# Gate and up weight chunks of a two-stage MoE layer: one 8 KB run per partition instead of four of 2 KB

## The reference, cut to what matters

```
h  = x + gmlp(rmsnorm(x) * norm_mix)
hn = rmsnorm(h) * norm_ffn
for each expert e:   y[e] = (silu(hn[rows_e] @ w_gate[e]) * (hn[rows_e] @ w_up[e])) @ w_down[e]
out = rmsnorm(h + sum_e weight_e * y[e]) * norm_final
```

## Time and profile before

| what | value |
|---|---|
| median of 3 executions | 1353.35 us (1352.79 to 1354.3) |
| span of the profiled execution | 1351.2 us |
| TensorE busy with matmuls | 937.8 us, 69% of the span |
| VectorE, ScalarE busy | 277.7 us and 293.4 us |
| bytes moved by DMA | 463.38 MB |
| mean rate over the span | 343 GB/s |

### The profile page before, as it was taken

The page is one execution under the profiler, slowest core; times in us unless marked ns, Lnnn a source line. Parts: engine busy times, 40 slices in busy tenths (PEclk is TensorE's granted clock), DMA queues, the critical chain, the costliest instruction groups (busy, mean ns, idle before and its releaser), DMA issues.

```text
span 1351.2 us, 18292 instructions
## 1 busy us (share of the span) xinstructions
PE 937.8 (69%) x7326; PEld 508.5 (38%) x7327; DVE 277.7 (21%) x471; ACT 293.4 (22%) x492; POOL 17.2 (1%) x53
## 2 busy tenths in 40 slices
PE   7999999995675766576666656656655656656664
PEld 6788788882232322132222223222222323223221
DVE  4454755442001000200020002000200110010003
ACT  5444555433111111111111110111111111111113
POOL 1100000002000000000000000000000000000000
PEclk9999999998777787777678788778988888688677
DMA  8776756765799999999999999999999999999993
GB/s 276 271 242 231 232 186 210 272 212 212 284 398 398 378 398 398 398 370 397 397 364 395 396 397 368 398 397 397 369 396 397 397 376 396 397 397 365 399 398 161
DMA packets 182361, 463.38 MB, mean 343 GB/s; under 512 B 7992, under 2 KB 8080, under 8 KB 165456
## 3 DMA queue, kind: packets, MB, share of 16 engines
q1 hardware_dynamic: 181520, 458.26, 90.7%
q0 software_dynamic: 624, 2.94, 0.6%
q10 hardware_dynamic: 80, 0.02, 0.0%
HBM read 459.09 MB, written 2.10 MB: 341 GB/s over the span
## 4 chain that ended last, share of the span: by engine, by line
PE 40%; SPq 22%; DMA 21%; issue 10%; DVE 3%; ACT 3%; DVEq 0%; ACTq 0%
SPq L234 22%; DMA late<-in_e_w_down 18%; PE bank L922 18%; PE bank L1062 8%; PE bank L1104 5%; PE bank L1046 5%; PE bank L1079 2%; DMA ring<-in_e_w_up 1%; DMA w_raw<-in_a_w_in 1%; PE bank L1051 1%; DVE xeT L847 1%; ACT w_router L578 1%; ACT y L590 1%; DVE w_lo L636 1%; PE bank L1010 1%
## 5 line engine op out<-in xcount | busy, mean ns | idle before, releaser
L1062 PE MATMUL bank<-ring,xeT 128*32 128x256 f32 x3584 | 237.6, 429 | 41.5 <-DVE xeT L847 31.3
L1046 PE MATMUL bank<-h,sel 128*32 128x512 f32 x512 | 115.6, 1053 | 180.4 <-issue 178.0
L1062 PEld LDWEIGHTS bank<-ring,xeT 128*32 128x32 f32 x3584 | 144.9, 123 | 127.9 <-issue 85.7
L922 PE MATMUL bank<-w_hi,xT_hi 128*128 128x512 f32 x384 | 155.3, 404 | 5.6 <-DVE w_lo L636 3.5
L922 PE MATMUL bank<-w_hi,xT_lo 128*128 128x512 f32 x384 | 151.5, 394 | 0.0
L922 PE MATMUL bank<-w_lo,xT_hi 128*128 128x512 f32 x384 | 151.1, 394 | 0.0
L636 DVE TENSOR_TENSOR w_lo<-w_raw,w_hi 128x1024 fp32r<-128x1024 f32 x96 | 119.2, 1242 | 132.5 <-ACT w_hi L431 132.3
L431 ACT CAST w_hi<-w_raw 128x1024 fp32r<-128x1024 f32 x96 | 100.9, 1051 | 140.9 <-PE bank L922 135.5
L590 ACT COPY y<-bank 32x512 f32<-32x512 f32 x128 | 73.8, 577 | 204.3 <-PE bank L1079 201.9
L1046 PEld LDWEIGHTS bank<-h,sel 128*32 128x32 f32 x512 | 19.5, 157 | 252.7 <-issue 250.2
L847 DVE TENSOR_TENSOR xeT<-bank,cols_T 128x512 f32<-128x512 f32 x32 | 22.1, 692 | 421.9 <-PE bank L1051 421.9
(11 more groups left out here) (148 smaller groups left out, 421.5 us busy)
## 6 DMA issues: line engine op xcount, KB each, us to landing
ring<-in_e_w_gate SPq DMA_DIRECT2D x112, 1024.0 KB, 14.4
ring<-in_e_w_up SPq DMA_DIRECT2D x112, 1024.0 KB, 14.9
ring<-in_e_w_down SPq DMA_DIRECT2D x64, 1024.0 KB, 14.8
late<-in_e_w_down SPq DMA_DIRECT2D x64, 1024.0 KB, 15.7
w_raw<-in_a_w_in SPq DMA_DIRECT2D x64, 512.0 KB, 3.7
w_raw<-in_a_w_out SPq DMA_DIRECT2D x32, 512.0 KB, 4.0
v<-in_e_w_gate SPq DMA_DIRECT2D x16, 1024.0 KB, 14.4
v<-in_e_w_up SPq DMA_DIRECT2D x16, 1024.0 KB, 14.7
```

Source lines behind the costliest of these rows:

```text
L922: ins = pe.matmul(Z[parity][t][:, :], a[:, k, toks], b[:, hc % 2, j, :], start=(k == 0 and part == 0), stop=(k == KD - 1 and part == 2))
L1046: ins = pe.matmul(XE[j * CAP:(j + 1) * CAP, :], sel[:, t, :], h[:, t, j * NBLK:(j + 1) * NBLK], start=(t == 0), stop=(t == NT - 1))
L1062: ins = pe.matmul(GU[c * CAP:(c + 1) * CAP, 0:256], xeT[:, kk, kc, :], slot_of(2 * kc + c // 2, q % 2)[:, half:half + 256], start=(kc == 0 ...
```

## The change

The source of a gate or up chunk is cut so that partition p receives the four adjacent rows 4p to 4p+3 of its 512 rows (8 KB in one run in memory), not rows p, 128+p, 256+p and 384+p (four runs of 2 KB). The destination is the same 8 KB per partition. So that features and weights meet, piece b of the transposed tokens must hold features 4p+b of each group of 512: the four transposes take every fourth column of xe, beginning at b, and norm_ffn is loaded a second time, as g_rows, in the matching order. The router keeps the old order.

```diff
+        g_rows = sb("g_rows", [P, NQ, KC])
...
+        g_rows_in = sem("g_rows_in")
...
                 w, k = (e_gate, e_up)[c % 2], c // 2
-                return w[0, e, k * KC * P:(k + 1) * KC * P, :].rearrange("(j p) n -> p j n", p=P)
+                return w[0, e, k * KC * P:(k + 1) * KC * P, :].rearrange("(p j) n -> p j n", j=KC)
...
             pool.dma_start(b_router[:, NGRP:NR], r_b_exp.partition_broadcast(P)).then_inc(router_in, 16)
+            pool.dma_start(g_rows[:, :, :], norm_ffn.rearrange("o (j p b) -> p (o j) b", j=NQ, b=KC)).then_inc(g_rows_in, 16)
             pool.wait_ge(lo_done, HC)
...
+                dve.wait_ge(g_rows_in, 16)
                 dve.wait_ge(s.xeT_ps, n + 1)
 
                 dve.tensor_tensor(xeT[:, :, :, :], TR[:, :].rearrange("p (b j c) -> p b j c", b=KC, j=NQ),
-                                  g_ffn.rearrange("p (j b) -> p b j", b=KC).unsqueeze(3).to_broadcast([P, KC, NQ, CAP]),
+                                  g_rows[:, :, :].rearrange("p j b -> p b j").unsqueeze(3).to_broadcast([P, KC, NQ, CAP]),
                                   ALU.mult).then_inc(s.xeT, 1)
...
                 for b in range(KC):
-                    ins = pe.transpose(TR[:, b * P:(b + 1) * P], xe[:, b * P:(b + 1) * P], ident[:, :])
+                    ins = pe.transpose(TR[:, b * P:(b + 1) * P], xe.rearrange("p (c b) -> p b c", b=KC)[:, b, :], ident[:, :])
                 ins.then_inc(s.xeT_ps, 1)
```

## The result

The changed kernel takes 1310.68 us (median of 4, 1307.6 to 1312.82), the kernel before 1353.07 us (4, 1350.22 to 1354.3). The ratio is 0.9686, interval 0.9666 to 0.9707: 3.1% faster, 42.4 us. Forecast were 1317.7 us and -35.6 us, range 1303 to 1330. The profiled execution took 1309.32 us for a span of 1307.4 us; the span of before was 1351.2 us, so the two traces differ by 43.8 us.

A forecast was written before the change was run, and what follows sets the result against it. The expert stage was taken to be bound by weight transfers, with DMA not the limit at group boundaries. Terms -49.5 + 11.6 + 2 + 0.3 = -35.6 us gave a span of 1315.6 and a time of 1317.7 us, range 1303 to 1330.

The forecast's parts named there:

- (1): Expert stage: gate and up chunks in 8 KB runs save 0.21 us each, -49.5 us; upper bound 0.23 us each.
- (2): Seven group boundaries: TensorE's path stays 29.6 us while the queue runs dry 1.65 us sooner; 11.6 us given back.
- (3): Four transposes per pass read xe with a step: 2 us at the boundaries; loads between 142 and 568 ns.
- that rival's 12 us: Strided transpose loads at the 7 boundaries cost their upper bound, 12 us instead of 2: 1328 us; chance 0.08.
- (4): New norm_ffn load on GpSimd's queue: issue hidden, its runs mix with the mixer's halves; +0.3 us, -0.5 to +0.9.
- (5): VectorE's new wait for g_rows: data there 300 us earlier, so nothing; the tail is unchanged too.
- (6): SP's queue: long issues become short, over 3 us vanish; issue to landing gets longer; worth nothing.
- The boundary doesn't bind: Group boundaries: loss comes from DMA engines' unequal ends, so 11.6 us aren't given back; about 1304 us; chance 0.10.
- Doesn't do what it says: Gate and up chunks still go out in 2 KB pieces, rate stays 387: 1353 us plus at most 2; chance 0.07.
- The slower rival: TensorE's start-up gaps grow behind larger descriptors; if both boundary gaps double, 75 us more, 1393 us; chance 0.05.

The follow-up runs named there:

- experiments 1 to 4: Changed kernel with 2 KB runs 1358.52 us, 4 KB 1323.51, 1 KB 1424.71; parts singly: source order 1311.15, all but it 1357.95, g_rows unused 1353.37.
- experiment 5: TensorE's scatter moved from before the next group's first gather to behind that pass's gate and up matmuls: kernel before 1344.36 us, kernel after 1293.89 us.
- experiment 4: Parts singly: changed source order alone 1311.15 us; all of the change but that order 1357.95; kernel before plus g_rows loaded, waited for, unused 1353.37.

## Why the prediction was right, point by point

*(1) 8 KB runs, -49.5 us.* Right in kind and place (experiments 1 to 4) and nearly in size. The rates are 387 and 420 as forecast; but from landing to landing, the median of a gate or up chunk in the trace went from 2.706 to 2.485 us, 0.221 us and not 0.206. Over 240 chunks that is 3.5 us more than the sum had. The prediction's own upper bound has a slip: 421 against 387 GB/s is 0.22 us per chunk and not 0.23, and its low end of 1303 us goes with 0.22.

*(2) The boundaries give back 11.6 us.* Right in mechanism, somewhat too large. In the stretch of 28 experts 224 chunks, each 0.221 us shorter, would have brought 49.5 us, and it became 39.9 us shorter: 9.6 us were given back, with the strided transposes in it. The windows say 10; experiment 5 returns 8.1 of it by the times (some 7 us uncertain) and 5.8 by the traces. Why it is less than the whole 1.65 us each time isn't shown. It isn't that TensorE's path became shorter (207.7 us in sum over the seven boundaries, 205.6 before), although TensorE's gaps, 31 ahead of the gathers and 7 ahead of the scatters, did shrink. They sum to 167.4 and 34.6 us after the change:

```profile
PE bank L1050 <- issue: 167.4, 31, 6.7
PE bank L1108 <- issue: 34.6, 7, 5.6
```

and to these before:

```profile
PE bank L1046 <- issue: 178.0, 31, 6.8
PE bank L1104 <- issue: 38.0, 7, 5.6
```

*(3) Strided transposes, 2 us.* The load takes 216 ns, between the ends of 142 and 568, so the Trainium skill's note (SBUF — State Buffer, Specifications) that each new 16-byte line costs agrees with the row; it costs half a load more, and the four elements' time of the upper bound isn't reached. The time of it is 1.6 to 7.0 us by experiment 4 with the old source order, so that rival's 12 us are shut out there; in the changed kernel the boundary paths are 2.0 us longer in sum than with the source order alone, one execution each. That is the forecast's 2 us, but not well settled, and 0.6 us of it at most is the loads' own time; the forecast had no term for the rest.

*(4), (5) The new load and the wait, 0.3 us and nothing.* Nothing speaks against them: g_rows alone is -0.1 us, between -3.7 and +2.8. The issue took GpSimd 0.75 us:

```profile
26.39 0.75 POOL L365 DMA_DIRECT2D g_rows<-in_norm_ffn  x1
```

*(6) SP.* Issues over 3 us became rare, 7 of the expert chunks' 384 where there were 59, but did not vanish as forecast: the one at 624.40 still took 6.08 us. The time from issue to landing became longer, as forecast.

In the span, the sum's 35.6 us came out as 43.8, 8.2 more. Term (1) has 3.5 us of that. The 240 chunks come to 53.0 us, so 9.2 us were lost again in all, where terms (2), (3) and (4) together had 13.9: the other 4.7 us. How these divide among the three isn't shown beyond what stands above. The forecast of the time was 7 us too high, inside its range, because the two errors went the same way.

*The rivals.* "The boundary doesn't bind" fell by the 9.6 us given back and by experiment 5: the boundary does bind. "Doesn't do what it says" fell by the packets. The slower rival fell in its sign: with all descriptors at 8 KB, the waits ahead of L1050 are 5.40 us in the mean where they were 5.74, and those ahead of the scatters 4.94 where they were 5.43. The rule that 512 B are enough for line rate (the Trainium skill, DMA: Bandwidth & Descriptors, Specifications) doesn't hold for this stream: 1 KB runs reach 350 GB/s, 83% of what 8 KB runs do.

## What to carry to other kernels

Where weights stream at the DMA engines' limit, give each partition one long run by dealing adjacent rows to it, and permute the other operand to match; four strided transposes a pass cost little against it, at most 7 us of 42 here. Price it from two windows of the trace that move runs of different length, not from the share of busy time, which was at or over 1 in both. Then look for the stretches where something else sets the pace: there a faster stream only empties the buffers sooner, and moving work off that path was worth more after the change (16.8 us) than before it (9.1).

## What the runs showed that I had not expected

- The cost of a run is linear from 1 to 8 KB: about 9 ns and 37.8 ns per KB on each DMA engine (46.7, 84.9, 160.8, 312 ns).
- One boundary of the kernel after moved only 272 GB/s in its window. TensorE's granted clock there was 0.68, against 0.82 to 0.93 in the windows of the others, and the path from last landing to next issue took 31.6 us instead of 28.6 to 30.0. A boundary on TensorE's path pays for the clock; a DMA-bound stretch doesn't, as the two windows at 420 GB/s with a granted clock of 0.51 and 0.89 show.
- With the scatter moved away, the two gaps of about 5 us became one of 13.3 to 14.2 us at the six boundaries where the program's loop goes back to its start, and one of 6.59 us at the one where it doesn't.
